# A two-block network on one Trainium2 core: bank-wise closing of row products, early second weight units, a chunk loop on three engines

## The reference

```python
def first_block(x, mem, ...):
    h = x
    for l in range(DEPTH):                      # 2 layers
        hn = rms_norm(h, norm_mix_pre[l])
        ...                                     # l = 0: RG-LRU; l = 1: sliding window over shared_k, shared_v
        mixed = jnp.concatenate([y, m_out], axis=-1) @ w_out[l]
        h = h + rms_norm(mixed, norm_mix_post[l])
        f = swiglu_ffn(rms_norm(h, norm_ffn_pre[l]), w_ffn_in[l], w_ffn_out[l])
        h = h + rms_norm(f, norm_ffn_post[l])
        if l == N_A_LAYERS - 1:
            kv = rms_norm(h, norm_kv) @ w_kv_shared
            ...
    return h

def swiglu_ffn(x, w_in, w_out):
    gu = x @ w_in
    g, u = gu[..., :D_FF], gu[..., D_FF:]
    return (jax.nn.silu(g) * u) @ w_out

def second_block(x, c, ctx, c_ctx, w_ada, ...):
    x = x + sincos_2d(rows, GRID_W)
    mod = jnp.split(jax.nn.silu(c) @ w_ada[l] + b_ada[l], N_MOD, axis=-1)
    h = modulate(rmsnorm(x, g_pre_mix[l]), shift1, scale1)
    y, yc = token_mix(h, hc, lp, with_ctx)      # projections z, u and x_m; mLSTM; Fourier mixing; w_out
    x = x + gate1 * rmsnorm(y, g_post_mix[l])
    h2 = modulate(rmsnorm(x, g_pre_ffn[l]), shift2, scale2)
    return x + gate2 * rmsnorm(hier_moe(h2, lp), g_post_ffn[l])   # 16 experts
```

## Time and profile before

| | |
|---|---|
| median of 3 runs | 1951.76 us (1950.09 to 1953.26) |
| span of the profiled execution | 1947.3 us |
| PE busy | 1814.3 us, 93% |
| DVE, ACT, POOL busy | 1216.2 (62%), 896.1 (46%), 125.7 (6%) |
| chain that ended last | PE 85%, DVE 7%, ACT 6% |

### The profile page before, as it was taken

The page is one execution under the profiler, slowest core; times in us unless marked ns, Lnnn a source line. Parts: engine busy times, 40 slices in busy tenths (PEclk is TensorE's granted clock), DMA queues, the critical chain, the costliest instruction groups (busy, mean ns, idle before and its releaser), DMA issues.

```text
span 1947.3 us, 25641 instructions
## 1 busy us (share of the span) xinstructions
PE 1814.3 (93%) x9201; PEld 1507.9 (77%) x9201; DVE 1216.2 (62%) x2170; ACT 896.1 (46%) x1452; POOL 125.7 (6%) x137
## 2 busy tenths in 40 slices
PE   7997999999999997899999999799987989999997
PEld 7875788888887865678888888678576878888885
DVE  3554668887323656456865532564575479889888
ACT  3446443222213445543223221342383368888885
POOL 1000000000000000000110000120000210110102
PEclk8898999999999998999999999799998879999999
DMA  4223225455333124024655423330011359999995
GB/s 150 87 76 115 87 64 142 134 145 147 107 96 96 44 65 184 23 65 137 182 159 149 119 93 97 112 89 22 21 67 66 108 222 377 395 385 370 386 372 187
DMA packets 203854, 289.32 MB, mean 149 GB/s; under 512 B 12332, under 2 KB 150548, under 8 KB 203636
## 3 DMA queue, kind: packets, MB, share of 16 engines
q1 hardware_dynamic: 188788, 239.56, 36.9%
q0 software_dynamic: 11920, 36.48, 6.1%
q10 hardware_dynamic: 3056, 12.06, 1.6%
HBM read 271.77 MB, written 21.53 MB: 151 GB/s over the span
## 4 chain that ended last, share of the span: by engine, by line
PE 85%; DVE 7%; ACT 6%; issue 1%; DMA 1%; POOL 0%; DVEq 0%; ACTq 0%; POOLq 0%
PE bank L200 23%; PE bank L202 23%; PE bank L201 23%; PE bank L69 11%; PE bank L654 2%; DVE weights_low L227 1%; PE bank L2195 1%; ACT weights_high L221 1%; DVE tmp L69 1%; DVE z_and_u L69 1%; DVE ring L69 1%; PE bank L1651 1%; ACT spare L69 1%; PE bank L2544 1%; PE bank L272 1%
## 5 line engine op out<-in xcount | busy, mean ns | idle before, releaser
L227 DVE TENSOR_TENSOR weights_low<-ring,weights_high 128x1024 fp32r<-128x1024 f32 x202 | 246.7, 1223 | 395.3 <-ACT weights_high L221 394.8
L200 PE MATMUL bank<-XH,weights_high 128*128 128x512 f32 x1056 | 423.2, 401 | 17.8 <-DVE weights_low L227 6.5
L202 PE MATMUL bank<-XH,weights_low 128*128 128x512 f32 x1056 | 415.6, 394 | 0.0
L201 PE MATMUL bank<-XL,weights_high 128*128 128x512 f32 x1056 | 415.2, 393 | 0.0
L221 ACT CAST weights_high<-ring 128x1024 fp32r<-128x1024 f32 x202 | 211.1, 1047 | 432.6 <-PE bank L202 422.8
L200 PEld LDWEIGHTS bank<-XH,weights_high 128*128 128x128 f32 x1056 | 200.8, 190 | 63.0 <-DVE weights_low L227 9.6
L202 PEld LDWEIGHTS bank<-XH,weights_low 128*128 128x128 f32 x1056 | 200.7, 190 | 43.4
L201 PEld LDWEIGHTS bank<-XL,weights_high 128*128 128x128 f32 x1056 | 201.1, 190 | 40.3 <-issue 0.5
L2235 DVE TENSOR_TENSOR XL<-ring,XH 128x1024 fp32r<-128x1024 f32 x144 | 169.8, 1219 | 11.7 <-ACT XH L2229 11.7
L2229 ACT CAST XH<-ring 128x1024 fp32r<-128x1024 f32 x144 | 145.2, 1048 | 0.6 <-PE bank L202 0.6
L69 DVE SCALAR_TENSOR_TENSOR squares<-ring,c_silu,squares 128x128 f32<-128x128 f32 x384 | 135.2, 352 | 13.6
(11 more groups left out here) (506 smaller groups left out, 3263.2 us busy)
## 6 DMA issues: line engine op xcount, KB each, us to landing
ring<-in_w_ffn_in SPq DMA_DIRECT2D x88, 512.0 KB, 4.7
ring<-in_w_gate SPq DMA_DIRECT2D x72, 512.0 KB, 5.4
ring<-in_w_up SPq DMA_DIRECT2D x72, 512.0 KB, 7.3
ring<-in_w_down SPq DMA_DIRECT2D x72, 512.0 KB, 5.9
ring<-in_w_ada POOLq DMA_DIRECT2D x48, 512.0 KB, 4.7
ring<-in_w_ffn_out SPq DMA_DIRECT2D x44, 512.0 KB, 3.6
ring<-in_w_out SPq DMA_DIRECT2D x24, 512.0 KB, 3.6
slot_output<-expert_out SPq DMA_DIRECT2D x18, 512.0 KB, 6.7
```

Of the source, the lines that this page charges most:

```text
L200: PE.matmul(out_ap, w_h, x_h, start=first, stop=False, skip_group_check=True)
L201: PE.matmul(out_ap, w_h, x_l, start=False, stop=False, skip_group_check=True)
L202: return PE.matmul(out_ap, w_l, x_h, start=False, stop=last, skip_group_check=True)
L227: V.tensor_tensor(wl[:, s, :], ring[s][:, :], wh[:, s, :].bitcast(F32), ALU.subtract).then_inc(split_done.sem, 1)
```

## The change

- **Closing.** `rows_closing` takes the last unit of w_out and w_ffn_out in another order: banks 0 to 3 with half 0, banks 0 to 3 with half 1, then banks 4 to 7 each with both halves. Slot 0 and slot 1 are reported used by the two products groups of bank 7.
- **rows_root.** The low part of the next first half is now subtracted ahead of the additions. DVE adds six squares, and PE sums two parts.
- **Waits.** Casts wait for the last user of their own slot (`slot_used`), not for a running count.
- **Early.** The second unit's weights of the first FFN, of the values, of the second FFN and of z and u are loaded into `ring[2]`, `ring[3]` and split into buffers of their own, during the closing unit (A), in FFN 0's output projection (B), in the second output projection's unit 2 (C), in FFN 1's output projection (D). Their units need no split then, and unit 2's halves take the common slots.
- **Transition.first_unit** replaces `Residual.chunks` in A, B and C. Squares are added in pairs on DVE, so PE has four groups of token sums; of the low parts six come from ACT (a scaled copy) and POOL (a subtraction), those of chunks 3 and 7 from DVE; the scaled chunks and some squares lie in banks.
- **Modulation** starts one unit later, and two of its loads are issued elsewhere.

```diff
             S.wait_ge(landed[s].sem, landed[s].n)
-            if g >= 2:
-                S.wait_ge(used_done.sem, g - 1)
+            if slot_used[s]:
+                S.wait_ge(used_done.sem, slot_used[s])
             S.copy(wh[:, s, :], ring[s][:, :]).then_inc(high_done.sem, 1)
...
+            slot_split[s] = split_done.n
+
+        def slots_used(*each):
+
+            for s in each:
+                used_done.n += 1
+                slot_used[s] = used_done.n
...
+        class Early:
+
...
+            def split(self, s, *after):
+                act.need(*after)
+                S.wait_ge(landed[2 + s].sem, landed[2 + s].n)
+                S.copy(self.high[:, s, :], ring[2 + s][:, :]).then_inc(self.high_line.sem, 1)
+                self.high_line.n += 1
+                V.wait_ge(self.high_line.sem, self.high_line.n)
+                V.tensor_tensor(self.low[:, s, :], ring[2 + s][:, :], self.high[:, s, :].bitcast(F32),
+                                ALU.subtract).then_inc(self.split_line.sem, 1)
+                self.split_line.n += 1
...
+                    if closing and i == units - 1:
+                        if s == 1:
+                            closing()
...
+                    elif early and i == 1:
+                        PE.wait_ge(early.split_line.sem, s + 1)
+                        products(i, s, False, early).then_inc(used_done.sem, 1)
+                        used_done.n += 1
+                        if not fused:
+                            open_half(src, s, 2)
...
+        def rows_closing(unit, xh, xl, ready=None, order=None, tokens=None):
+
+
+            def closing():
+                for s, c in (*((0, c) for c in range(4)), *((1, c) for c in range(4)),
+                             *((s, c) for c in range(4, KC) for s in range(2))):
+                    row = order[2 * unit + s] if order else 2 * unit + s
+                    if c == 0:
+                        if ready:
+                            PE.wait_ge(ready.sem, row + 1)
+                        if tokens:
+                            pe.need(tokens[row])
+                        PE.wait_ge(split_done.sem, slot_split[s])
+                    last = three_pass(bank[c][:, :], wh[:, s, c * P:(c + 1) * P], wl[:, s, c * P:(c + 1) * P],
+                                      xh[:, row, :], xl[:, row, :], False, False)
+                    if c == KC - 1:
+                        last.then_inc(used_done.sem, 1)
+                    elif s == 1:
                         last.then_inc(chunk_done.sem, 1)
                         chunk_done.n += 1
-                return last
-            return products
+                slots_used(0, 1)
+            return closing
...
             if next_src:
                 load_half(next_src, 0, 0)
                 split_high(0)
+                split_low(0)
...
                     added[c] = vec.do(V.tensor_tensor, total, squares[0], squares[1], ALU.add,
                                       after=[squared[0], squared[1]])
-                elif 1 < c < KC - 2:
+                elif 1 < c < KC - 1:
                     added[c] = vec.do(V.tensor_tensor, total, total, squares[c % 4], ALU.add,
...
             if next_src:
-                split_low(0)
                 load_half(next_src, 0, 1)
                 split_high(1)
             pe.need(m0)
-            parts = ((squares[(KC - 2) % 4], squared[KC - 2]), (squares[(KC - 1) % 4], squared[KC - 1]),
-                     (total, added[KC - 3]))
+            parts = ((total, added[KC - 2]), (squares[(KC - 1) % 4], squared[KC - 1]))
             for n, (part, ready) in enumerate(parts):
                 pe.need(ready)
                 for t in range(TT):
                     tok = pe.do(PE.matmul, bank[0][:, t:t + 1], part[:, t * P:(t + 1) * P], ones[:, 0:1],
-                                start=n + t == 0, stop=n == 2, skip_group_check=True)
+                                start=n + t == 0, stop=n == 1, skip_group_check=True)
             if floor is None:
...
+        class Transition(Residual):
...
+            def first_unit(self):
...
+                scaled, squared, paired, summed, high, low = {}, {}, {}, {}, {}, {}
+                moved = {0: tmp[:, 0, :], 1: tmp[:, 1, :], **{k: bank[k][:, :] for k in range(2, KC)}}
+                squares = (sq[:, 0, :], spare[:, 1, :], *(bank[k][:, :] if k % 2 else sq[:, k // 2 % 2, :] for k in range(2, KC)))
+                halves = [slice(0, T // 2), slice(T // 2, T)]
+                whole_of = (kept, tmp[:, 0, :], tmp[:, 1, :])
...
+                        bank_free[k] = [scaled[k]]
+
+                def add(k, cols=slice(0, T)):
+                    x_ready[k] = [vec.do(V.tensor_tensor, X[:, k, cols], X[:, k, cols], moved[k][:, cols], ALU.add,
+                                         after=[scaled[k], *x_ready[k]])]
...
+                def square(k):
+                    squared[k] = act.do(S.activation, squares[k], X[:, k, :], ACT.Square,
+                                        after=[*x_ready[k], *([summed[k - 4]] if k in (4, 6) else [])])
...
+                def pair(k):
+                    dst = sq[:, k // 2 % 2, :]
+                    paired[k] = vec.do(V.tensor_tensor, dst, squares[k], squares[k + 1], ALU.add,
+                                       after=[squared[k], squared[k + 1]])
...
+                def lows(k):
+                    if k in (3, last):
+                        V.wait_ge(act.line.sem, high[k][1])
+                        low[k] = vec.do(V.scalar_tensor_tensor, XL[:, k, :], X[:, k, :], self.next_gain[:, k:k + 1],
+                                        XH[:, k, :].bitcast(F32), ALU.mult, ALU.subtract)
+                    else:
+                        whole = whole_of[k % 4]
+                        act.do(S.activation, whole, X[:, k, :], ACT.Copy, scale=self.next_gain[:, k:k + 1],
+                               after=[low[k - 4]] if k >= 4 else [])
+                        G.wait_ge(act.line.sem, act.line.n)
+                        low[k] = pool.do(G.tensor_tensor, XL[:, k, :], whole, XH[:, k, :].bitcast(F32), ALU.subtract)
...
+                for k in range(1, KC):
+                    if k < last:
+                        scale(k + 1)
+                    add(k)
+                    highs(k)
+                    if k == 4:
+                        lows(3)
+                    if k != 3:
+                        lows(k)
+                    square(k)
+                    if k in (3, 5, 7):
+                        pair(k - 3)
...
+                    if 1 <= k - 1 < last - 1 or k == 1:
+                        if k != 4:
+                            pe.need(low[k - 1])
+                            for s in range(2):
+                                one_pass(s, wh, XL, k - 1)
+                    if k == 5:
+                        pe.need(low[3])
+                        for s in range(2):
+                            one_pass(s, wh, XL, 3)
+                    if k in (3, 5, 7):
+                        sums(k - 3)
...
-        ada_steps = ([[], []] + [[n] for n in range(20)],
-                     [[], []] + [[n, n + 1] for n in range(20, 36, 2)] + [[n] for n in range(36, 48)])
-        def ffn(l, residual, next_src, beside=None):
+        ada_steps = ([[], [], []] + [[n] for n in range(17)] + [[17, 18], [19]],
+                     [[], [], []] + [[n, n + 1] for n in range(20, 38, 2)] + [[n] for n in range(38, 48)])
...
+            if (i, s) == (3, 1):
+                early.split(0, used_done.now(), vec.line.now())
+                early.split(1)
...
+        unit_at = 191616
+        early = Early("first_ffn", ffn_src(0), 1, unit_at)
+        early.load(used_done.now())
+        spread = mix_out(I["w_out"][0], ffn_src(0), row_order, row_ready, row_part)
+        G.wait_ge(early.split_line.sem, 2)
         modulation_load(0)
         modulation_load(1)
...
+            if (i, s) in ((9, 1), (10, 0)):
+                values_early.split(2 * i + s - 19, used_done.now())
...
+        def split_early(i, s):
+            if i == 2:
+                early.split(s, used_done.now())
...
+        G.wait_ge(early.split_line.sem, 2)
+        modulation_load(20)
+        modulation_load(21)
...
+            if (i, s) in ((8, 1), (9, 0)):
+                zu_early.split(2 * i + s - 17, used_done.now())
```

176 lines of the change are left out of this document (132 added, 44 removed).

## The result

The change makes the kernel slower. In the first comparison the median was 1970.6 us (1967.6 to 1972.4, 4 runs) against 1950.9, a ratio of 1.0097 (95% interval 1.0083 to 1.0112), that is +18.9 us by the ratio (the medians are 19.7 apart). The forecast was +11.25 us, a ratio of 1.0058, and a median of 1963.0 in a range of 1953 to 1971: the right side and the right mechanism of the loss, a size that is too small, and a time just inside the range.

What follows compares the result with a forecast made beforehand. TensorE, busy 93% of the span, was taken as the bound, so its work or pauses decide. Gains of 17.95 us against losses of 29.2 made 11.25 slower: 1963.0 on the median of 1951.76, range 1953 to 1971.

Steps and rivals of the forecast that it cites:

- A: Pause from first output projection to first FFN: 6.7 us lost there, 4.0 gained in its chunk loop.
- B: Pause from first FFN to keys and values: 7.8 us lost there, 5.5 gained in its chunk loop.
- C: Pause from second output projection to second FFN: 7.8 us lost as in B, 4.0 gained in its loop as in A.
- part 1: Closing unit, A to D: late slot release delays cast and squares; scale at T0 + 12.6 to 12.7, 29.2 us lost.
- T0: At each pause, the end of the closing unit's last product; other times are counted from it.
- part 2: Chunk loop in A, B, C: takes 16.7 us, between 16.0 and 17.3; gains 4.0, 5.5 and 4.0.
- R3: Rival, slower still: GpSimd stretches VectorE's additions in three loops, 8 us, 1971 (1 to 2 by the skill's rule); chance 0.13.
- part 3: Early second units no longer wait for weights: 4.3 us gained, less 0.85 charged in B.
- D: Pause from second FFN to the second block: 6.9 us lost.
- E: Pause from second block's output projection to its router: no next weights cast, one sum group less, up to 1.0 us gained.
- R1: Rival, no change: TensorE keeps full clock across A to D, 2.5 us less each, net +0.9, about 1953; chance 0.15.
- R2: Rival, faster: R1 plus loops at ACT's bound without lower clock, 1946; or ACT not holding squares, about 1930; chance 0.08.

Runs made afterwards that it cites:

- e1: Changed kernel with the eight squares ahead of the cast and subtraction of the next first half in rows_root; 1935.9 us, ratio 0.9911 to before.
- e3: Kernel before with the bank-wise closing order alone, old running counts kept; 1976.3 us, ratio 1.0112.
- e9: e1 with products on a tile of zeros added behind the token sums and the spread of the root in A to D; 1938.3 us, ratio 0.9915.
- e11: e9 with the token sums of chunks 0 to 3 issued ahead of the low products in the chunk loop; 1929.6 us, ratio 0.9882.
- e7: e1 without the four early units, their halves split in the common slots as before; 1953.5 us, ratio 1.0012.
- second profile: The changed kernel itself run and profiled once more, nothing edited; 1968.3 us against 1952.9, ratio 1.0067.
- e2: Changed kernel with the closing unit walked half by half again, all else kept; 1954.0 us, ratio 1.0006.
- e5: e2 with the old rows_root: five additions, low-half subtraction behind them, three sum groups; 1937.6 us, ratio 0.9937.

## Why the prediction was right, and where its sizes were off

**The closing (part 1): right, in each step.** The cast at T0 - 0.65 was -0.59; the squares behind it at +0.40 were +0.36; the last addition at 6.15 was 6.29; a sum group at the lower clock 1.87, 1.84; the scale at 12.6 to 12.7 was 12.73 to 13.15. The four losses were 6.8, 8.0, 7.9 and 7.4, together 30.1, for the 29.2 forecast. e1 and e3 show that it is the late release of the slot, with the cast ahead of the squares, that does it: e3 adds the late release alone and loses 26.6, e1 takes the cast out of the way alone and gets the pauses back. C was taken as B and is 4.79 before (B 4.87).

**The chunk loop (part 2): too large, 13.5 for 8.7.** The loops took 18.04, 17.82 and 19.00 in the first profile (gains 2.7, 4.4, 1.6) and 18.1, 18.8 and 18.2 in the second (together 8.6). I had put them at 16.7, between two bounds of 16.0 and 17.3. The step that failed is the lower one. I added up ACT's instructions as if nothing stood between them; two of the squares wait for TensorE's sums, 1.9 us in all in A, 1.6 in B and 2.8 in C, so that the chain runs through three engines and not one. e9, at the full clock, still had 17.7; e11, which shortens these two waits, 16.6. So the 16.7 that I took needs both the full clock and the sums issued earlier, and the changed kernel has neither. The rest over 17.7 is the lower clock at the loop's start, for which I had taken only what the shorter pause of before had cost. In C it lasted to 883, a good six us.

**R3 did not come.** Its number, 1971, is near the first median, but that is luck: its stretched additions are not there. GpSimd's subtractions took 1.3 us (the first 1.8), not 1.70. Here are two of them in A of the changed kernel with DVE's instructions beside them:

```profile
254.55 0.68 DVE L69 TENSOR_TENSOR X<-X,tmp 128x512 f32<-128x512 f32 x1
254.55 1.82 POOL L69 TENSOR_TENSOR XL<-spare,XH 128x512 fp32r<-128x512 f32 x1 [19.92 <-ACT spare L69]
...
256.68 1.29 POOL L69 TENSOR_TENSOR XL<-tmp,XH 128x512 fp32r<-128x512 f32 x1 [0.30 <-ACT tmp L69]
...
257.06 0.68 DVE L69 TENSOR_TENSOR X<-X,bank 128x512 f32<-128x512 f32 x1
...
257.66 0.85 DVE L69 TENSOR_TENSOR squares<-squares,spare 128x512 f32<-128x512 f32 x1
```

The addition that reads a bank is not stretched (0.68), the pair of two SBUF tiles is, by 0.17 (when it started, 0.31 us of GpSimd's instruction were left). But the addition of chunk 1, of two SBUF tiles as well, took 0.68, and there GpSimd's instruction is the longer one, 1.82 for 1.29. The rule of the Trainium skill that the prediction weighed (GPSIMD Engine Reference, Key points) names contention between the two engines for such an instruction. The trace agrees with that, but not with the prediction's reading that it is always VectorE that pays, and the price is small: one pair in each loop, 0.2 us, where the prediction's estimate was 1 to 2 in all.

**The early units (part 3): right in the waits, and short of the clock.** I took 4.3 less 0.85 in the stretches behind the loops and in D. They gave 1.6 + 3.1 + 2.6 + 0.1 = 7.4 in the first profile and some 2.5 in the second. The stall that I priced at 0.85 in B's closing unit was there, 0.91:

```profile
623.26 0.47 PE L200 MATMUL bank<-hidden_high,weights_high 128*128 128x512 f32 x1 [0.91 <-DVE weights_low L226]
```

The term that was too small is the clock behind the loops, which I had left at nothing. These are the 15 us behind A's loop, first of the kernel before, then of the changed one:

```profile
262.70:277.70 15.00, 14.19 (x58) 11.38 (x59) 5.30 (x9) 4.29 (x7) 0.00 (x0) 0.89 0.25 71
...
272.10:287.10 15.00, 15.00 (x72) 12.55 (x72) 4.72 (x8) 5.27 (x7) 0.00 (x0) 1.00 0.17 49
```

B and C read 0.91 and 0.89 before, and 1.00 in the first profile of the changed kernel. In the second it is 0.89 again behind A and C, so this gain comes in one execution and not in another. e7 points the same way: its waits alone explain half of the 17.6 us.

**E** gave 1.1 in the first profile and nothing in the second, where the lower clock fell into it. **The modulation** and its loads show nowhere.

**Adding up.** First profile: 30.1 lost in the pauses, 0.3 by the first product, which stands 2.42 behind the scale instead of 2.31; less 8.7 (loops), 7.4 and 1.1; then 5.2 ahead of A and 0.3 elsewhere: 18.7. The touched places alone are +13, near the forecast of 11.25, and that nearness is luck: the loops gave 4.8 less than I took and the early units 4.0 more. In the second profile, whose stretches between the places gained less, they are +19. How much of the difference between +13.1 and +18.9 in the two comparisons belongs to the change and how much to the clock's luck the runs do not tell.

**R1 (the clock stays full)** was clearly wrong: the first sum group took 1.84 in A, B and C of the first profile and in all four places of the second, and the spread 2.04 to 2.05 everywhere. R1's own sum has a slip: 2.5 less in each of four places leaves 19.2 of the losses, not 18.8, and a net of +1.3. **R2's** second way, that ACT does not hold the squares, is excluded by the same timeline; e1 shows what it would have given.

## What to carry to other kernels

When products are put in another order, ask of each buffer that they read when it is released now, then what stands at the head of the queue that waits for it, and what stands behind that. The queue's order can be the same, word for word, and the pause twice as long. And when work for TensorE is taken out of a pause, ask whether what is left still covers the other engines: two idle microseconds in each of five places cost 14 here (e2 against e5), and products that compute nothing can be free (e9).
